# Packing small parameters into three arrays, moving their loads to SyncE, and interleaving squares with sigmoids in a fused transformer kernel

## The reference

```python
def first_block(x, p, positions, ...):
    cos, sin = rope_tables(positions)
    h = x
    for i in range(2):
        z = rms_norm(h, g_mix[i]) @ w_in[i]
        z_a, z_b, z_c = split_cols(z, (A_COLS, B_COLS, C_COLS))
        y_a = chunked_spatial_gating(z_a, gm_ln_g[i], gm_ln_b[i], gm_ws[i], gm_bs[i])
        y_b = rwkv7_time_mix(z_b, ...)
        y_c = nsa_attention(z_c, cos, sin, ...)
        h = h + jnp.concatenate([y_a, y_b, y_c], axis=-1) @ w_out[i]
        hn = rms_norm(h, g_ffn[i])
        h = h + (swiglu(hn, ...) if i == 0 else moe_swiglu(hn, router_w, router_b, ...))
        gate = jax.nn.sigmoid(rms_norm(h, g_ple[i]) @ ple_gate_w[i])
        h = h + (p[i] @ ple_proj_w[i]) * gate
    return rms_norm(h, g_final)
# second_block: per layer swiglu, three attentions (one with bias rel_bias_table_2), gated merge, swiglu
```

## Time and profile before

| | |
|---|---|
| median of 3 runs | 3214.26 us (3207.21 to 3215.03) |
| the profiled execution's own time | 3212.79 us |
| its span, first to last instruction | 3211.0 us |
| PE busy | 2907.2 us, 91% |
| PE weight load | 2459.9 us, 77% |
| DVE busy | 2066.3 us, 64% |
| ACT busy | 1550.3 us, 48% |
| mean granted clock of PE | 0.933 of full speed |
| HBM | 187 GB/s over the span |

### The profile page before, as it was taken

One profiled execution on the slowest core, in us unless ns is written; L12 is line 12 of the kernel. 1 busy time (PEld: TensorE's weight loads), 2 busy tenths in 40 slices (PEclk: granted clock), 3 DMA queues, 4 the chain that ended last, 5 costly groups with the idle time before them and its releaser, 6 DMA issues. The chain is left out here.

```text
span 3211.0 us, 46033 instructions
## 1 busy us (share of the span) xinstructions
PE 2907.2 (91%) x17806; PEld 2459.9 (77%) x17806; DVE 2066.3 (64%) x2936; ACT 1550.3 (48%) x2377; POOL 20.9 (1%) x22
## 2 busy tenths in 40 slices
PE   5788997978799999999998999869999999869998
PEld 5666886965677777777876788749888888749887
DVE  3444772445398888988893765475476765475476
ACT  3224442324277777777783434354343434354343
POOL 0000000010000000000000000000000000000000
PEclk9778998976899999999999999879999999979999
DMA  6401553300378887888884456215454455215451
GB/s 243 146 28 53 209 185 120 117 2 1 159 306 353 316 345 307 359 319 335 313 346 182 168 194 208 75 37 208 157 197 170 184 191 198 78 46 211 152 189 59
DMA packets 107520, 599.00 MB, mean 187 GB/s; under 512 B 26117, under 2 KB 34395, under 8 KB 38505
## 3 DMA queue, kind: packets, MB, share of 16 engines
q1 hardware_dynamic: 99288, 591.01, 48.9%
q10 hardware_dynamic: 8080, 5.89, 0.6%
HBM read 593.94 MB, written 6.12 MB: 187 GB/s over the span
## 5 line engine op out<-in xcount | busy, mean ns | idle before, releaser
L2319 DVE TENSOR_TENSOR expert_w_low<-weight_ring,expert_w_high 128x1024 fp32r<-128x1024 f32 x528 | 629.8, 1223 | 75.2 <-ACT expert_w_high L2263 64.3
L715 PE MATMUL psum<-hnT_parts,weight_high 128*128 128x512 f32 x1760 | 620.5, 395 | 0.2
L2263 ACT ACTIVATE expert_w_high<-weight_ring 128x1024 fp32r<-128x1024 f32 x528 | 552.0, 1057 | 94.9 <-PE psum L2192 53.1
L717 PE MATMUL psum<-hnT_parts,weight_low 128*128 128x256 f32 x1760 | 493.1, 280 | 0.0
L769 DVE TENSOR_TENSOR weight_low<-weight_ring,weight_high 128x1024 fp32r<-128x1024 f32 x330 | 384.8, 1219 | 12.4 <-ACT weight_high L763 12.4
L715 PEld LDWEIGHTS psum<-hnT_parts,weight_high 128*128 128x128 f32 x1760 | 331.0, 188 | 75.1 <-DVE hnT_parts L457 1.2
L540 PE MATMUL psum<-hnT_parts,slab_high 128*128 128x256 f32 x2016 | 368.7, 285 | 12.8 <-DVE slab_low L583 12.5
L717 PEld LDWEIGHTS psum<-hnT_parts,weight_low 128*128 128x128 f32 x1760 | 331.4, 188 | 3.9
L763 ACT ACTIVATE weight_high<-weight_ring 128x1024 fp32r<-128x1024 f32 x330 | 324.7, 1045 | 8.7 <-PE psum L734 8.6
L540 PEld LDWEIGHTS psum<-hnT_parts,slab_high 128*128 128x128 f32 x2016 | 313.9, 191 | 14.5 <-DVE slab_low L583 13.9
L583 DVE TENSOR_TENSOR slab_low<-weight_ring,slab_high 128x2048 fp32r<-128x2048 f32 (+3 forms) x104 | 195.2, 1885 | 201.3 <-ACT slab_high L575 201.3
(11 more groups left out here) (395 smaller groups left out, 4601.2 us busy)
## 6 DMA issues: line engine op xcount, KB each, us to landing
weight_ring<-in_moe_w SPq DMA_DIRECT2D x264, 1024.0 KB, 6.8
weight_ring<-in_w_in SPq DMA_DIRECT2D x52, 1024.0 KB, 6.7
weight_ring<-in_ffn_w_gate SPq DMA_DIRECT2D x44, 1024.0 KB, 4.8
weight_ring<-in_ffn_w_up SPq DMA_DIRECT2D x44, 1024.0 KB, 6.4
weight_ring<-in_ffn_w_down SPq DMA_DIRECT2D x44, 1024.0 KB, 4.8
weight_ring<-in_ffn_w SPq DMA_DIRECT2D x33, 1024.0 KB, 4.8
weight_ring<-in_w_gate SPq DMA_DIRECT2D x24, 1024.0 KB, 4.8
weight_ring<-in_w_branch SPq DMA_DIRECT2D x24, 512.0 KB, 3.5
```

Of the source, the lines that this page charges most:

```text
L715: nc.tensor.matmul(out, hi[:, kt, :], hn[2][:, kt, :, :], start=(kt == 0), stop=(kt == KT - 1), skip_group_check=True)
L717: last = nc.tensor.matmul(out[:, 0:SEQ], lo[:, kt, :], hn[0][:, kt, :], start=False, stop=(kt == KT - 1), skip_group_check=True)
L2263: nc.scalar.activation(part(0, k, half), raw(c, k, half), ACT.Copy).then_inc(high[k].sem, 1)
L2319: nc.vector.tensor_tensor(part(1, k, half), raw(c, k, half), as_f(part(0, k, half)), ALU.subtract).then_inc(low[k].sem, 1)
```

## The change

The host lays out the 128-wide vectors as two arrays (`cols1`, `cols2`, already in columns) and every parameter of a layer that is one tile high as one array `params` (128 partitions x 2504 per layer, 10 KB a partition; `gm_ws` and `p` already transposed). The kernel loads these instead of the many small ones. SP issues all of it, in the order: `h`, kept constants, `cols1`, slabs 0 and 1, `params`, `bs`, positions, other constants, table, `cols2`, slabs 2 to 8. The product of the bias table moves to the end of layer 0's project stage, with its write to HBM and a wait for that write ahead of `write_scratch`. The rope steps move behind n = 7 (DVE) and n = 10 (ACT). Layer 1's parameters are issued by SP at the end of layer 0's ple stage. The squares of the ple stage are taken between its sigmoids, one part behind.

```diff
 class Core:
-        self.cols1 = self.sb("cols1", [P, P])
-        self.cols2 = self.sb("cols2", [P, P])
+        self.cols1 = self.sb("cols1", [P, vec_width(VEC1)])
+        self.cols2 = self.sb("cols2", [P, vec_width(VEC2)])
+        self.rope_step, self.bias_step = sig("rope_step"), sig("bias_step")
 def load_sqrt(K):
-    K.nc.scalar.activation(K.root_warm[:, :], K.c("ones")[:, 0:1], ACT.Sqrt)
+    K.nc.scalar.activation(K.root_warm[:, :], K.eps[:, 0:1], ACT.Sqrt)
+PARAMS = (("ln", 2 * SEQ), ("ws", RH * P), ("lora_up", SEQ), ("g_up", SEQ), ("gn", 2 * P), ("cmp_w2", 2 * HD),
+          ("pT", 2 * SEQ), ("router", KT * NE), ("router_b", NE))
+def params_of(inputs, l):      # on the host: the parts side by side, broadcast or transposed
...
 def setup_stage: the vector loads, memsets, transposes, copies, bias product and ACT's loads are gone
+    dve = Steps(K.dve_step, ["eps"])
+    late = [(K.const1[:, :], arg["shape_consts"][:, KEPT_W:CONST_W]), (T.table[:, :], arg["rel_bias_table_2"]),
+            (K.cols2[:, :], arg["cols2"])]
+    loads = T.loads(arg, 0)
+        def _(sp):
+            sp.dma_start(K.h[:, :, :], ...).then_inc(K.inputs_in.sem, 16)
+            sp.dma_start(K.const[:, :], arg["shape_consts"][:, 0:KEPT_W]).then_inc(K.inputs_in.sem, 16)
+            sp.dma_start(K.cols1[:, :], arg["cols1"]).then_inc(K.inputs_in.sem, 16)
+            for n in range(2):
+                W.load(sp, n)
+            for dst, src in loads + late:
+                sp.dma_start(dst, src).then_inc(K.params_in.sem, 16)
+            for n in range(2, SLOTS):
+                W.load(sp, n)
+            W.next = SLOTS
+        def _(v):
+            nc.vector.memset(K.eps[:, :], EPS).then_inc(*dve.mark("eps"))
+        def _(a):
+            a.wait_ge(*dve("eps"))
+            load_sqrt(K)
+            a.wait_ge(*K.inputs_in(3))
+            for blk in range(NBLK):
+                for half in range(2):
+                    add_square(K, blk, half, 2, K.bank[4 + 2 * blk + half][:, :])
 def write_scratch(K, T, sp):
-    sp.wait_ge(*K.scratch_io(0))
+    sp.wait_ge(*K.bias_step(2))
+    sp.dma_start(arg["bias_scratch"], T.bias_rows[:, :]).then_inc(K.scratch_io.sem, 16)
+    sp.wait_ge(*K.scratch_io(1))
     moves = ...                     # three transfers, as before
 Block1Tensors.loads:
+        out = [(self.params[:, :], arg["params"][l]), (self.bs[:, :], row_to_all(arg["gm_bs"], l * RH * P, RH * P, 1))]
         if l == 0:
+            out.append((self.pos_i[:, :], row_to_all(arg["positions"], 0, SEQ)))
-def layer_params_stage(K, T, layer): ...
 rope_programs:
-        v.wait_ge(*K.params_in(0))
 GatedMlp:
-    def turn(self, t, bank): ...     # transposes of gm_ws on PE
         if n == 3:
-            v.wait_ge(*self.pe("w_turned"))
-            nc.vector.tensor_tensor(T.wsT[:, :, :], bank[:, :].rearrange("p (h t) -> p h t", t=P), upto, ALU.mult)
+            v.wait_ge(*self.K.params_in(0))
+            nc.vector.tensor_tensor(T.wsT[:, :, :], T.wsT[:, :, :], upto, ALU.mult)
 project_stage, PE:
-                    if n == 7:
-                        pe.wait_ge(*gmlp.dve("w_masked"))
-                    if n == 1:
-                        gmlp.turn(pe, K.bank[7])
                 gmlp.mix(pe, mixed)
+                if first_layer:
+                    pe.wait_ge(*K.params_in(0))
+                    pe.wait_ge(*stored(6))
+                    nc.tensor.matmul(K.bank[6][0:12, :], T.table[:, :], K.c("bucket"), start=True, stop=True).then_inc(K.bias_step.sem, 1)
 project_stage, ACT:
                 S.high(act, 1)
-                if first_layer:
-                    rope_by_scalar(act)
                 for n in range(12):
                     S.high(act, n + 2)
+                    if n == 10 and first_layer:
+                        rope_by_scalar(act)
 project_stage, DVE:
                 S.low(v, 1)
-                if first_layer:
-                    rope_by_vector(v)
                 for n in range(12):
                     S.low(v, n + 2)
+                    gmlp.by_vector(v, n)
+                    if n == 7 and first_layer:
+                        rope_by_vector(v)
                 gmlp.finish(v, mixed)
+                if first_layer:
+                    v.wait_ge(*K.bias_step(1))
+                    nc.vector.tensor_copy(T.bias_rows[:, :], K.bank[6][0:12, :]).then_inc(K.bias_step.sem, 1)
 ple_stage, SP:
+                if following:
+                    sp.wait_ge(*pe(("proj", n_slabs - 1)))
+                for dst, src in following:
+                    sp.dma_start(dst, src).then_inc(K.params_in.sem, 16)
 ple_stage, PE and DVE: the transposes of p (L2440) and their copy (L2477) are gone
 ple_stage, ACT:
+                for i in every:
+                    if i == count - 1:
+                        squares(i - 1)
+                    sigmoid(i)
+                    if 0 < i < count - 1:
+                        squares(i - 1)
+                load_sqrt(K)
+                squares(count - 1)
```

More of the change, by code:

```diff
@@ L303, in vec_at, with vec_width, vec_columns @@
     raise KeyError(name)
[L306 to L310, removed]
+def vec_width(table):
+    return NLAYER * sum(rows for _, rows in table)
+def vec_columns(inputs, table):
+    return np.concatenate([np.asarray(inputs[name]).reshape(-1, P).T for name, _ in table], axis=1)
+PARAMS = (("ln", 2 * SEQ), ("ws", RH * P), ("lora_up", SEQ), ("g_up", SEQ), ("gn", 2 * P), ("cmp_w2", 2 * HD),
+          ("pT", 2 * SEQ), ("router", KT * NE), ("router_b", NE))
@@ new lines @@
+PARAMS_W = sum(width for _, width in PARAMS)
+def params_of(inputs, l):
+    get = lambda name: np.asarray(inputs[name])[l]
+    over = lambda row: np.broadcast_to(row.reshape(1, -1), (P, row.size))
+    heads = [get(name).reshape(2, 2, HD) for name in ("rw_gn_g", "rw_gn_b")]
+    gn = [np.broadcast_to(np.concatenate([t[:, par].reshape(-1) for t in heads])[None, :], (RC, 2 * P)) for par in range(2)]
+    parts = {
+        "ln": np.concatenate([over(get("gm_ln_g")), over(get("gm_ln_b"))], axis=1),
+        "ws": get("gm_ws").transpose(2, 0, 1).reshape(P, RH * P),
+        "lora_up": np.concatenate([get("rw_w_up"), get("rw_a_up")], axis=0),
+        "g_up": get("rw_g_up"),
+        "gn": np.concatenate(gn, axis=0),
+        "cmp_w2": np.concatenate([get("nsa_kc_w2"), get("nsa_vc_w2")], axis=1),
+        "pT": get("p")[0].T.reshape(2, P, SEQ).transpose(1, 0, 2).reshape(P, 2 * SEQ),
+        "router": np.asarray(inputs["router_w"])[0].reshape(KT, P, NE).transpose(1, 0, 2).reshape(P, KT * NE),
+        "router_b": over(np.asarray(inputs["router_b"])[0]),
+    }
+    return np.concatenate([parts[name] for name, _ in PARAMS], axis=1)
@@ L313, in row_to_all, with setup_stage @@
 def row_to_all(t, offset, n, parts=P):
     return bass.AP(tensor=t.tensor, offset=offset, ap=[[0, parts], [1, n]])
-def setup_stage(K, params, bias_rows):
+def setup_stage(K, T):
     nc, arg, W = K.nc, K.arg, K.weights
[L322 to L384, removed]
@@ L878, in __init__ @@
         self.sin = sb("sin", [P, SEQ])
-        self.wsT = sb("gm_wsT", [P, RH, P])
+        self.table = sb("bias_table", [32, 12])
+        self.bias_rows = sb("bias_rows", [12, 512])
     def new_mixer(self, K, ctx):
@@ L1087, in _ @@
                 if first_layer:
[L1088 removed]
+                    write_scratch(K, T, sp)
             @block.tensor
@@ L2436, in gates @@
                     last.then_inc(*pe.mark(("gate", i)))
-                for kt in range(2):
-                    for b in range(NBLK):
-                        last = nc.tensor.transpose(K.bank[7][:, kt * SEQ + b * P:kt * SEQ + (b + 1) * P],
-                                                   T.ple[:, b, kt * P:(kt + 1) * P], K.c("ident"))
-                last.then_inc(*pe.mark("p_turned"))
                 t.wait_ge(*W.arrived(first + n_slabs))
-                t.wait_ge(*dve("pT"))
                 proj(0)
@@ L2463, in _, with sigmoid, squares @@
                     norm.whole(a, kt)
-                for i, (n, blocks, bank) in enumerate(parts):
+                def sigmoid(i):
+                    n, blocks, bank = parts[i]
                     a.wait_ge(*pe(("gate", i)))
                     nc.scalar.activation(gate[:, n, over(blocks)], K.bank[bank][:, over(blocks)], ACT.Sigmoid).then_inc(*act.mark(("gate", i)))
-                load_sqrt(K)
-                for i, (n, blocks, bank) in enumerate(parts):
+                def squares(i):
+                    n, blocks, bank = parts[i]
                     a.wait_ge(*K.h_added(i + 1))
@@ L3022 @@
     arrays["in_shape_consts"] = consts
+    for name, table in (("cols1", VEC1), ("cols2", VEC2)):
+        arrays[f"in_{name}"] = np.ascontiguousarray(vec_columns(inputs, table))
+    arrays["in_params"] = np.stack([params_of(inputs, l) for l in range(NLAYER)])
     for name, a in arrays.items():
```

102 lines of the change are left out of this document (37 added, 65 removed).

## The result

The changed kernel takes 3189.97 us (median of 5 runs, 3184.32 to 3192.07) against 3214.26 (5 runs, 3207.21 to 3216.63): the ratio is 0.9923, with a 95% interval of [0.9912, 0.9935]. It is faster, by 24.3 us, where the forecast had 40; 3190 lies above the range of 3166 to 3184. Timed again beside the variants the median was 3187.43 (6 runs), the ratio 0.9909 [0.9891, 0.9927]. The profiled execution has a span of 3188.7 us; PE is busy for 2905.7 (91%), DVE 2064.3 (65%), ACT 1551.2 (49%), the same shares as before to a point.

What follows compares the result with a forecast made beforehand. PE, busy nearly all the time, was taken as the bound, so only its waits could give. Terms -13.5 - 12.8 + 6.0 - 3.0 - 5.6 - 9.7 - 0.4 = -39.0 led from 3212.8 to 3173.8, forecast 3174 us, range 3166 to 3184.

Steps and rivals of the forecast that it cites:

- the price of SP's slab issues in the first stage: Before the first barrier: seven slab issues at the median 0.56 us each, bringing SP from 6.0 to 9.9 us.
- Start: First stage, up to the norm: with fewer loads before the squares the norm begins at about 10.1 instead of 23.63, -13.5 us.
- rival (a): First stage: SP holds the first barrier, slab issues at 1.37 us each give back 5.7 us, total 3180; chance 0.11.
- Rope and parameters: Layer 0's project stage: PE's gap between products 1 and 2 goes, product 2 ends at 48.64 instead of 61.45, -12.8 us.
- Bias product: End of layer 0's project stage: product, copy, write and issues stand uncovered, stage ends at 135.6 instead of 129.65, +6.0 us.
- Ple starts: Start of both ple stages: without the transposes and the copy PE starts the projection earlier, -1.5 us each, -3.0 together.
- Squares: End of both ple stages: one square instead of eight remains behind the table load, -2.8 us each, -5.6 together.
- rival (b): Both ple stages: the squares swap tables, so ACT loads twice and comes 0.7 to 2.8 us late, 3175 to 3180; chance 0.05.
- Layer parameters: Seam between layer 0's ple and layer 1's project stage: ACT's block of DMA issues goes, 555.86 becomes 545.82 + 0.3, -9.7 us.
- gm_ws: Layer 1: the transposes of `gm_ws`, 0.4 us between two products, go, -0.4 us.
- Rival (c): Start of rwkv stage: scratch transfers, about 17 us of DMA, delay instruction fetches; three in a row make 3225; chance 0.02.
- rival (d): Seam after layer 0's ple stage: SP comes late to the barrier behind its slabs, 3184 if all 9.7 are lost; chance 0.05.

Runs made afterwards that it cites:

- x5_bias_mid: The kernel after with the bias product behind product 9 of project0 and DVE's copy of it behind that of product 10; 3180.31 us, ratio 0.9896.

## Why the prediction was wrong

By 3212.8 + the seven stages' measured -27.7 (mean of two traces each) the forecast should have read 3185; the untouched stages put 3.5 on top. The step that failed most was the price of SP's slab issues in the first stage, 6.9 us. By itself it would have left the forecast in its range, at 3181; two smaller failures, in ple1 and in the row norm behind it, and the untouched stages took the time out of it. Step by step:

- **Start: -6.6 instead of -13.5.** This step failed, and rival (a) with its chance of 0.11 was the true case. Loads, table and squares came as worked out. (The sum has a slip of 0.1: 9.9 and 0.3 are 10.2, so -13.4.) The slab issues were priced at the median 0.56, though the same row had one of 1.37; they took 1.47 each, and SP's end at 16.6 is beyond even my worst case of 15.6. The length of these issues is no price of the instruction: three of the seven took 0.43 us, and the other four waited for room in the queue. The very rows of ACT had a sign: two issues in 5.61 us by an engine that waited for nothing else. By the packets, some 1060 rows of ACT's queue were unmoved when each of the two returned. I took the time as the cost of those loads, and put eighteen DMAs with some 2200 rows on one queue ahead of a barrier. Not every long issue is explained by that: the one of 1.37 us ended with some 510 rows of its own queue unmoved, while ACT issued too, and no run shows what held it.
- **Rope and parameters: -13.3 at the end of product 2, -11.9 at the end of the mix, instead of -12.8.** Right. From the start of the stage product 2 ends at 24.6 us (41.52 - 16.92) where it was 37.9. The steps moved to n = 7 cost nothing, as forecast. Of the gain 1.45 us goes in the last product: from DVE's copy of product 10 to ACT's store of product 11 it is 8.4 us where it was 6.9, with the granted clock at 0.60 (from 92 to 100 us) instead of 0.70 (from 112 to 120). The term had nothing for that.
- **Bias product: +5.5 instead of +6.0.** Right. The write took 1.54 us from its issue to the next, less than the 2.4 assumed, and 1.76 in `x5_bias_mid`. The Trainium skill's fixed 2.0 us for a DMA (DMA: Bandwidth & Descriptors, "Anatomy of one DMA — SWDGE (gpsimd) path"), which that section gives for the path of GpSimd, is more than this write took from SP, and its late update to HBM is not seen in either trace.
- **Ple starts: -1.5 in layer 0 as forecast, 0 in layer 1.** ple0 with the old squares is 43.76 against 45.26 (46.76 in the second trace, which has 4.6 us of the stage at 1.2 GHz where the first has 0.7). In ple1 the step failed: I carried a row of layer 0 to layer 1 without reading what PE waits for there.
- **Squares: -2.79 each.** Right, to 0.01. No table load stands between a sigmoid and a square, so rival (b) is out. The trace agrees with the sentence of ScalarE: Activation LUTs in the Trainium skill ("Table sets: the hidden batching unit") that cheap functions are in every set, though the square isn't among its examples. It again shows no drain behind a load: the load takes 1.28 us, and the next activation is 1.29 us after its start.
- **What was not in the sum: +2.6 in the row norm.** Its gain rows are issued at the stage's own start, behind two slabs that are released by ple1's last products. With squares ending earlier the issue followed 2.2 us behind them, and DVE waited 5.49 us. Half of the squares' term went there. The trace of before had the sign: DVE waited 2.70 us for the same rows there, and the second slab ahead of them took 6.8 us to land, to 1766.9, past the issue of the rows at 1765.03.
- **Layer parameters: -9.8 for -9.7, gm_ws: -0.8 for -0.4.** Right. SP's issues did not hold the ple barrier; rival (d) is out.
- **Rival (c) is out**: the scratch transfers now run under rwkv_inputs, which is 21.44 us long in every trace.
- **The other stages: +3.5.** Not forecast, and not settled. The clock's fall to 1.2 GHz comes at other points of rwkv, attention and moe_route from one kernel to the next; moe_route stands at 16.3 in nine of twelve traces of after and its variants, against 13.8 and 14.4 in before. That this belongs to the change isn't shown, since three variants with edits elsewhere have 13.8 to 14.5. The cause of these 3.5 us stays open.

In numbers, by the means of two traces: 39.0 forecast, less 6.9 (SP's issues), 2.6 (gain rows), 2.5 (ple1: 1.5 for its start as forecast, the rest a projection that starts some 0.4 later and runs slower) and 0.6 (project0), plus 1.3 that ple0, the layer parameters and `gm_ws` gave beyond their terms, is 27.7; the untouched stages take 3.5: 24.2. The medians show 24.3, and timed again 27.8 (3215.20 to 3187.43); that the first agrees to 0.1 is luck.

## What to carry to other kernels

An issue that takes long can be a queue that is full of rows. Before DMAs are gathered on one queue, count their rows as well as their bytes, and put nothing behind them, a barrier least of all, that the next stage waits for: the bulk loads go behind the barrier. When an engine's last work before a barrier is shortened, read what the next stage waits for first, for a transfer issued at that barrier doesn't come earlier by as much. And a saving found in one layer's rows is to be looked up in each other layer's, where another wait may cover it.

## What the runs showed of the hardware that I had not expected

- A DMA issue blocks by rows: 512 rows of 64 bytes held SP for 5.31 us behind a full queue, four single rows for 1.20.
- A wait of PE can cost more than the idle time in it: of the 6.07 us before ple1's projections only 3.1 could be filled, and the stage got 5.9 us shorter, since it then ran at 2.4 GHz throughout instead of 6.8 us at 1.2.
- Stages that an edit does not touch can differ by up to 5 us each from trace to trace (rwkv_chain 50.5 to 55.4, moe_route 13.8 to 16.3). The time at 1.2 GHz differs with them: 9.5 to 17.9 us in rwkv_chain, 11.0 to 16.3 in moe_route.
